# Attention of a hybrid layer: value products and row sums taken by three key tiles instead of by one

## The reference

```python
def _block_attention(q, k, v):
    qb = jnp.moveaxis(q.reshape(B, nb, Q_BLOCK, AT_KV_HEADS, AT_GROUP, D), 1, 0)
    def one(qblk):
        s = jnp.einsum('bqkgd,bskd->bkgqs', qblk, k).astype(jnp.float32) * scale
        p = jax.nn.softmax(s, axis=-1).astype(v.dtype)
        return jnp.einsum('bkgqs,bskd->bqkgd', p, v)
```

## Time and profile before

| | |
|---|---|
| Time, median of 3 runs | 2375.9 us (2374.77 to 2378.68) |
| Profiled execution: its time / its span | 2374.82 us / 2373.0 us |
| PE busy over the span | 2295.2 us (97%) |
| DVE, ACT, POOL busy | 1426.0 (60%), 805.5 (34%), 224.7 us (9%) |
| Granted TensorE clock, mean | 0.991 of full |
| Maxima of the heads, L2476 | 1.36 us each, 64 of them |
| Loop over query tiles | from about 1161.4 to 1396.15 us of the span |

### The profile page before, as it was taken

How to read it: one execution, slowest core, us unless ns; L and a number is a source line. 1 busy time by engine, 2 the same in 40 slices (tenths; PEclk the granted TensorE clock), 3 DMA queues, 4 the chain that set the end, 5 groups by cost and what they waited for, 6 DMA issues and landing times. The chain is left out here.

```text
span 2373.0 us, 43700 instructions
## 1 busy us (share of the span) xinstructions
PE 2295.2 (97%) x17959; PEld 2029.6 (86%) x17959; DVE 1426.0 (60%) x2212; ACT 805.5 (34%) x1398; POOL 224.7 (9%) x245
## 2 busy tenths in 40 slices
PE   6999999999999899998899999998999999999997
PEld 5887779999999889998655569877999999998886
DVE  5331266533555467665677646768676676677877
ACT  5321132213333233223344444325223222234444
POOL 0000000001110011112222101000111121120001
PEclk9999999999999999999999999999999999999999
DMA  6324632235452532214101138421222222259434
GB/s 279 120 85 182 225 112 107 100 135 202 155 173 86 198 107 87 83 66 158 44 19 48 56 112 312 154 92 59 79 104 91 76 107 91 73 183 271 129 98 124
DMA packets 126877, 295.60 MB, mean 125 GB/s; under 512 B 19808, under 2 KB 63280, under 8 KB 117376
## 3 DMA queue, kind: packets, MB, share of 16 engines
q1 hardware_dynamic: 98112, 238.67, 29.9%
q10 hardware_dynamic: 24640, 39.46, 4.5%
q0 software_dynamic: 3968, 15.21, 1.7%
HBM read 207.83 MB, written 85.53 MB: 124 GB/s over the span
## 5 line engine op out<-in xcount | busy, mean ns | idle before, releaser
L62 PE MATMUL ps<-prj_w,h_hi 128*128 128x512 f32 (+1 forms) x864 | 254.2, 378 | 4.2 <-DVE h_lo L755 4.2
L62 PE MATMUL ps<-h_hi,fill_whi 128*128 128x384 f32 x672 | 235.8, 351 | 4.7 <-ACT fill_st L1119 2.4
L62 PE MATMUL ps<-h_lo,fill_whi 128*128 128x384 f32 x672 | 226.6, 337 | 3.5 <-issue 3.5
L62 PE MATMUL ps<-wt 128*128 128x320 f32 (+2 forms) x1046 | 227.2, 327 | 2.3 <-DVE merged L3308 1.3
L62 PE MATMUL ps<-h_hi,fill_wlo 128*128 128x384 f32 x672 | 226.5, 337 | 0.0
L62 PE MATMUL ps<-ys,mergedr 128*128 128x256 f32 (+1 forms) x1056 | 219.9, 297 | 0.4 <-issue 0.4
L62 PE MATMUL ps<-zb,mergedr 128*128 128x320 f32 (+2 forms) x764 | 199.8, 326 | 4.9 <-issue 2.7
L62 PE MATMUL ps<-zb,wt 128*128 128x384 f32 (+3 forms) x758 | 200.2, 325 | 0.0
L62 PEld LDWEIGHTS ps<-prj_w,h_hi 128*128 128x128 f32 x864 | 157.3, 190 | 43.0 <-issue 10.6
L62 PEld LDWEIGHTS ps<-wt 128*128 128x128 f32 x1046 | 179.6, 189 | 16.6 <-issue 2.6
L62 PEld LDWEIGHTS ps<-ys,mergedr 128*128 128x128 f32 x1056 | 174.6, 191 | 0.7 <-issue 0.7
(11 more groups left out here) (512 smaller groups left out, 4654.1 us busy)
## 6 DMA issues: line engine op xcount, KB each, us to landing
wraw<-in_w_ffn_in SPq DMA_DIRECT2D x22, 1024.0 KB, 5.1
prj_raw<-in_w_ada SPq DMA_DIRECT2D x16, 1024.0 KB, 5.9
fill_raw<-in_w_fill SPq DMA_DIRECT2D x30, 512.0 KB, 4.4
wtf<-a_dram SPq DMA_DIRECT2D x55, 256.0 KB, 2.7
bg_dram<-fill_st ACTq DMA_DIRECT2D x72, 192.0 KB, 2.0
xf<-bg_dram POOLq DMA_DIRECT2D x24, 576.0 KB, 7.4
tok_dram<-prj_tst ACTq DMA_DIRECT2D x45, 256.0 KB, 2.1
prj_raw<-in_w_tok SPq DMA_DIRECT2D x10, 1024.0 KB, 7.3
```

The costliest lines, as they stand in the source:

```text
L62: mm = pe.matmul(out, lhs[a], rhs[b], start=first and n == 0, stop=last and n == 2, skip_group_check=onto)
```

## The change

`values` and `sums` take three key tiles per visit, at `j` = 3 (tiles 0 to 2), 6 (3 to 5) and 8 (6 to 8). All nine key tiles are summed by ones on PE; `pair_up` and `pair_sums` are gone, and the ring `pt` has 6 tiles in place of 5 and two pair buffers. `shift_scores(i + 1, j - 1)` stands straight behind the scores at `j` = 1 to 8, one at each. `spread_sums(i - 1)` moves from `j` = 2 to 6, and `shifts(i + 1, 1)` comes last in the tile, behind the last sums.

On VectorE `inverted(i - 1)` moves behind the maximum of head 0, `normed(i - 1)` behind that of head 5, `norm_b` to the tile's start, `norm_a` one tile earlier at head 5, both splits to the tile's end, `ahead` to head 5 of the last tile. A copy of the rotation table (L2433) is gone. On GpSimd the rotation comes at the tile's start, with the power for the next one behind it. SyncE issues `queries_in(i + 5)` ahead of the wait for `norm`.

```diff
-    RING = 5
-    PAIRS = 3
-    PAIR_DONE, P_DONE = (1, 2, 4), (3, 5, 6)
-    PAIR_AT = (4, 6, 8)
+    RING, TRIO = 6, 3
...
             def shifts(i, kv):
                 pe.wait_ge(sem["nm"], AH * i + G * kv + G)
                 pe.wait_ge(sem["pte"], turn(i, 2 + kv))
-                if kv == 0 and i >= 2:
+                if kv == 1 and i >= 2:
                     pe.wait_ge(sem["norm"], i - 1)
...
+            def values(i, g):
+
+                if g == 0:
                     if i:
                         pe.wait_ge(sem["evict"], i)
                     else:
                         pe.wait_ge(sem["b0ev"], 24)
+                for j in range(TRIO * g, TRIO * g + TRIO):
+                    n = NT * i + j
+                    pe.wait_ge(sem["ex"], 2 * n + 2)
+                    for kv in range(KV):
+                        mm = pe.matmul(ps[kv * HD:kv * HD + HD, OB, :], va[:, j, kv, 0:HD], pt[n % RING][:, kv, :],
+                                       start=j == 0, stop=j == NT - 1)
                 mm.then_inc(sem["pv"], 1)
...
+            def sums(n):
+
+                i, g = divmod(n, NT // TRIO)
+                if g == 0 and i:
+                    pe.wait_ge(sem["rc"], i)
+                for x in range(TRIO):
+                    mm = add(pt[(TRIO * n + x) % RING], g == 0 and x == 0, g == 2 and x == TRIO - 1)
                 mm.then_inc(sem["sums"], 1)
...
                     if more and j < 2:
                         queries(i + 1, j)
-                    if i and j == 2:
-                        spread_sums(i - 1)
+                    if more and j >= 1:
+                        shift_scores(i + 1, j - 1)
                     if more and j == 5:
                         shifts(i + 1, 0)
-                    if more and 1 <= j < NT - 1:
-                        shift_scores(i + 1, j - 1)
-                    if j:
-                        values(i, j - 1)
-                    if j in PAIR_AT:
-                        pair_sums(i, PAIR_AT.index(j))
-                    if j >= 7:
-                        sums(i, j - 1)
-                    if more and j == NT - 2:
-                        shift_scores(i + 1, AH - 1)
+                    if j == 3:
+                        values(i, 0)
+                        sums(3 * i)
+                    if j == 6:
+                        if i:
+                            spread_sums(i - 1)
+                        values(i, 1)
+                        sums(3 * i + 1)
+                    if j == 8:
+                        values(i, 2)
+                        sums(3 * i + 2)
                 if more:
                     shifts(i + 1, 1)
-                values(i, NT - 1)
-                sums(i, NT - 1)
...
             def exponentials(i, j):
                 n = NT * i + j
                 if n >= RING:
-                    o, oj = divmod(n - RING, NT)
-                    act.wait_ge(sem["pv"], n - RING + 1)
-                    if oj < 2 * PAIRS:
-                        act.wait_ge(sem["paired"], PAIRS * o + oj // 2 + 1)
-                    else:
-                        act.wait_ge(sem["sums"], (NT - PAIRS) * o + P_DONE[oj - 2 * PAIRS])
+                    act.wait_ge(sem["sums"], (n - RING) // TRIO + 1)
...
             def tile(i):
 
-                if i >= 1:
-                    inverted(i - 1)
+                if i == -1:
+                    norm_a(3)
+                if 0 <= i < NT - 3:
+                    norm_b(i + 3)
                 for h in range(AH):
                     if i < LAST:
                         shift(i + 1, h)
                     if i >= 1 and h == 0:
+                        inverted(i - 1)
+                    if i == LAST and h == 5:
+                        ahead()
+                    if i >= 1 and h == 5:
                         normed(i - 1)
-                    if i >= 0 and h in (1, 3, 5):
-                        pair_up(i, h // 2)
-                    if 0 <= i < NT - 3 and h == 2:
-                        norm_a(i + 3)
-                    if 0 <= i < NT - 3 and h == 3:
-                        norm_b(i + 3, qtab[:, i + 2])
-                    if 0 <= i + 2 <= LAST and h == 5:
-                        next_split(i + 2, 0)
+                    if 0 <= i < NT - 4 and h == 5:
+                        norm_a(i + 4)
                 if i + 2 <= LAST:
+                    next_split(i + 2, 0)
                     next_split(i + 2, 1)
-                if i == LAST:
-                    ahead()
```

More of the change, by code:

```diff
@@ L1905, in attention @@
             pt = [over(f"pt{i}", [P, KV, G * P]) for i in range(RING)]
-            pair = [over(f"pair{i}", [P, KV, G * P]) for i in range(2)]
         k2 = ph.sb("k2", [P, NT, KV, HD])
@@ L1909, in attention @@
         kpart = [ph.sb("kparthi", [P, NK, KV, 2 * HD], F32R), ph.sb("kpartlo", [P, NK, KV, H1], F32R)]
-        r1, r2 = ph.sb("r1", [P, NT - 1, KV, HD // 2]), ph.sb("r2", [P, NT - 1, KV, HD // 2])
         va = ph.sb("va", [P, NK, KV, H1])
@@ L1916, in attention @@
         qtab = ph.sb("qtab", [P, NT - 1, 4, HD // 2])
+        r1, r2 = ph.sb("r1", [P, NT - 1, KV, HD // 2]), ph.sb("r2", [P, NT - 1, KV, HD // 2])
         q = ph.sb("q", [P, AH, HD])
-        qtb = ph.sb("qtb", [P, 4, HD // 2])
         q2, qn, qr = (ph.sb(n, [P, AH, HD]) for n in ("q2", "qn", "qr"))
@@ L1932, in attention @@
         names = ("load qload const knd kpow kout ktm kte qd qpow rope cpart qtm qte csmm cmx cex cptm cpte comm cdone "
-                 "part s1 mx nm ptm pte s2 ex pv sums paired rc spread norm evict yout0 yout1 kv dve mly mlw mlhi b0y1 b0y2 b0w b0yh b0wh b0yl b0wl b0mm b0ev b0out0 b0out1 b0out2 b0out3 b0out4 b0out5 b1lo")
+                 "part s1 mx nm ptm pte s2 ex pv sums rc spread norm evict yout0 yout1 kv dve mly mlw mlhi b0y1 b0y2 b0w b0yh b0wh b0yl b0wl b0mm b0ev b0out0 b0out1 b0out2 b0out3 b0out4 b0out5 b1lo")
         sem = {n: ph.sem(n) for n in names.split()}
@@ L1989, in _ @@
             for i in range(LAST + 1):
+                if i + 5 < NT:
+                    queries_in(i + 5)
                 sp.wait_ge(sem["norm"], i + 1)
                 rows_out(i + 1)
-                if i + 5 < NT:
-                    queries_in(i + 5)
                 if i == 3:
@@ L2011, in _, with inverse_norm, rope @@
             gp.tensor_tensor(krs[:], kms[:], khalf[:], ALU.pow).then_inc(sem["kpow"], 1)
[L2012 to L2017, removed]
+            def inverse_norm(n):
+                gp.wait_ge(sem["qd"], 4 * n + 3)
                 gp.tensor_tensor(qrs[:], qms[:], khalf[:, 0:AH], ALU.pow).then_inc(sem["qpow"], 1)
+            def rope(n, e):
                 gp.wait_ge(sem["qd"], 4 * n + 4 + 4)
@@ L2021, in rope @@
                 o = qr[:].rearrange("p h (d e) -> p h d e", e=2)
-                w = lambda c: qtb[:, c, :].unsqueeze(1).broadcast_to([P, AH, HD // 2])
-                for e in range(2):
[L2024 to L2032, removed]
+                w = lambda c: qtab[:, n, c, :].unsqueeze(1).broadcast_to([P, AH, HD // 2])
+                a, b = (0, 1) if e == 0 else (2, 3)
+                gp.tensor_tensor(u1[:], x[:, :, :, 0], w(a), ALU.mult).then_inc(sem["rope"], 1)
+                gp.tensor_tensor(u2[:], x[:, :, :, 1], w(b), ALU.mult).then_inc(sem["rope"], 1)
+                gp.wait_ge(sem["rope"], 6 * n + 3 * e + 2)
+                gp.tensor_tensor(o[:, :, :, e], u1[:], u2[:], ALU.subtract if e == 0 else ALU.add).then_inc(sem["rope"], 1)
+                gp.wait_ge(sem["rope"], 6 * n + 3 * e + 3)
+            inverse_norm(0)
+            for n in range(2):
+                inverse_norm(n + 1)
+                for e in range(2):
+                    rope(n, e)
+            inverse_norm(3)
+            for i in range(LAST + 1):
+                if i + 2 <= LAST:
+                    rope(i + 2, 0)
+                    rope(i + 2, 1)
+                if i + 3 <= LAST:
+                    inverse_norm(i + 4)
         def turn_queries(pe, kv, bank):
@@ L2161, in values @@
                         pe.wait_ge(sem["b0ev"], 24)
-                for kv in range(KV):
-                    mm = pe.matmul(ps[kv * HD:kv * HD + HD, OB, :], va[:, j, kv, 0:HD], pt[n % RING][:, kv, :],
-                                   start=j == 0, stop=j == NT - 1)
+                for j in range(TRIO * g, TRIO * g + TRIO):
[4 more added lines that the diff above has]
+                                       start=j == 0, stop=j == NT - 1)
                 mm.then_inc(sem["pv"], 1)
@@ L2171, in add @@
                                        start=first and kv == 0, stop=last and kv == KV - 1)
-                mm.then_inc(sem["sums"], 1)
[L2174 to L2183, removed]
+                return mm
+            def sums(n):
[4 more added lines that the diff above has]
+                    mm = add(pt[(TRIO * n + x) % RING], g == 0 and x == 0, g == 2 and x == TRIO - 1)
+                mm.then_inc(sem["sums"], 1)
             def spread_sums(i):
@@ L2188, in spread_sums @@
```

(16 more changed lines are left out.)

## The result

| | before | after |
|---|---|---|
| median of the runs, us | 2375.34 (4 runs, 2373.34 to 2378.68) | 2407.24 (4 runs, 2403.64 to 2411.2) |
| ratio, with its 95% interval | | 1.0133 (1.0119 to 1.0148) |
| profiled execution, us (span) | 2374.82 (2373.0) | 2411.2 (2409.4) |
| mean granted clock of the span | 0.991 | 0.985 |
| first scores of the loop to the end of its last sums, us | 234.35 | 271.96 |

The changed kernel is 31.9 us slower by the medians and 36.4 by the two profiled executions; the profiled one after is the slowest of its four runs. The loop alone is 37.6 us longer. What lies ahead of it and behind it is 1.2 us shorter together: the loop starts 0.46 earlier, and 976.1 us follow it instead of 976.85.

What follows compares the result with a forecast made beforehand. PE's written order was taken to bound the loop: 2.1 for tile 0, 19.4 for tiles 1 to 6 and 4.8 for tile 7 made +26.3, so 2374.8 + 26.3 = 2401 us; range 2389 to 2410, its own 2394 to 2408.

Steps and rivals of the forecast that it cites:

- the sum: Attention loop: +2.1 for tile 0, +19.4 for tiles 1 to 6, +4.8 for tile 7, so +26.3 us.
- the walk of waits: PE's order in a steady tile, start by start: five waits for maxima of 3.9 us, tile 33.4 instead of 30.2.
- a slow clock at 2408: Rival: the clock falls as PE waits some 4 us per tile and idles in tile 7; 2408, chance 0.03.
- The bound and the mechanism: Attention loop: PE's written order sets the time; head scores without value products between them wait for maxima, 2.2 us cycle.
- Tile 0: First loop tile, without reciprocal or spread: 31.5 us from its opening transposes, tile 1 starting 2.1 later.
- A steady tile: Tiles 1 to 6: 33.42 us each, together +19.4 over the former 181.12.
- The prediction's list beside its walk: Steady tile, 33.4 from 30.2: waits 3.9, restarts 0.5, opening 0.4, against 0.9 less work and 0.35 formerly waited.
- The pieces: PE prices in the loop: inner value product 0.88, sums 0.46, 0.46 and 0.55, visit of three about 4.2 us.
- The covers: Remaining VectorE work, GpSimd's 6 us and moved SyncE issues stay hidden; the opening waits 0.4 for ScalarE's copy.
- Tile 7: Last tile, no head scores: PE waits for exponentials, 28.7 us instead of 23.86, so +4.8.
- The rest: Outside the attention loop nothing moves; the loop's gain or loss goes into the total whole.
- The clock: Attention loop: a fall of PE's granted clock was a rival at 0.03, since no row of the loop showed it.

Runs made afterwards that it cites:

- the kernel with pairs: Against the changed kernel: four pairs back on VectorE, five sums, value visits of 1, 3, 3, 2, heads spread, last tile ordered as before; 2371.13 us, ratio 0.9986.
- the run with the wait filled: The changed kernel with five 512-column matmuls, product thrown away, added ahead of head 2 in tiles 1 to 6; 2406.94 us, ratio 1.0129.
- the reciprocal first: The changed kernel with the reciprocal of the row sums moved ahead of the maximum of head 0; 2398.33 us, ratio 1.0106.
- the heads apart: The changed kernel with head scores spread: five at j = 1, 3, 4, 6, 7, heads 2, 5, 7 inside visits; 2387.94 us, ratio 1.006.
- the one with another tile 7: The changed kernel with value products one key tile at a time in the last query tile alone, spread at j = 2 there; 2400.19 us, ratio 1.0104.

## Why the prediction came out as it did

It forecast 2401 and slower; 2407.24 is slower by a fifth more than that (31.9 us against 26.3 in the sum). Only part of the closeness is merit. Without the clock the loop would have grown by 25.0 us (below), to 2400, so the walk of waits was right almost to the microsecond. That 2407.24 still lies inside 2394 to 2408, by 0.8, is luck: that range was meant for spacing and restarts, not for the clock, which took 12.6 us in the profiled execution. The wider 2389 to 2410 takes in a slow clock at 2408, an estimate of mine for tile 7 alone. No run shows that term; in its place the profiled execution showed falls in five tiles, 12.6 us together and 4.9 of them in tile 7 (below). Step by step:

- *The bound and the mechanism: right.* Five waits for maxima a tile were forecast for five intervals, 3.9 us, the longest 1.67 behind head 1. The view lists 28 in seven tiles, four a tile; the fifth, from head 4 to 5, is too short to be drawn as idle time. Counted from starts (0.24 behind the last matmul of the scores) the five of tile 2 are 0.67, 1.50, 0.72, 0.23 and 0.63, together 3.75 (forecast 0.66, 1.67, 0.68, 0.19 and 0.68, together 3.88); the weight side waits 28.2 us in all, 4.0 a tile. The experiments gave prices: reciprocal 0.8, order of the heads 2.0 with the reciprocal's in it.
- *Tile 0: right.* 31.5 walked, 31.47 measured, +2.10.
- *A steady tile: right within 0.2.* 33.42 walked, 33.24 where the clock held. Over six tiles that is 1.1 less than the sum had. The prediction's list beside its walk doesn't add up: 30.2 with 3.9, 0.5 and 0.4 more and 0.9 and 0.35 less is 33.75, 0.3 above the walk. The work that falls away is the item too small there: from starts, and with 0.5 of restarts taken off, tile 2 has 28.5 us of work against 29.7 before (0.1 of restart off), 1.2 less and not 0.9. The sum goes by the walk, which has it right.
- *The pieces: right.* An inner value product was taken at 0.88; from the visit shown of tile 2, (1239.55 - 1236.82 - 1.01) / 2 = 0.86. Three sums take 1.44 (1239.55 to 1240.99), as 0.46 + 0.46 + 0.55 = 1.47. The visit is 4.17 to 4.18, and 4.12 behind the spread. A lone value product takes 0.15 more from start to start than an inner one (1.01 against 0.86); no run here shows what that difference is made of.
- *The covers: right.* `normed`, `norm_b`, splits and GpSimd hold up nobody, and the wait for ScalarE's copy at the opening is 0.31 in the view and 0.46 from starts (0.4 forecast), though the kernel with pairs shows how near `normed` is: behind one maximum more it costs 1.5 us a tile.
- *Tile 7: the walk fits, the clock not in it.* 28.7 was walked and 33.36 measured. PE waits for exponentials six times, 3.9 us in all. What the clock cost is below, and without it some 28.5 are left, which no run shows by itself.
- *The rest: right within 1.2 us.* Nothing outside the loop is slower.
- *The clock: wrong, and this is the mis-sized term.* The forecast gave it a chance of 0.03, with the reason that no row of the loop before showed it. No row of the loop could: before, PE had no wait there like those that the walk itself had just found. But the trace of before shows it 20 us ahead of the loop, where PE has such waits. Behind waits of 1.41 and 0.69 us head scores take 1.10 instead of 0.79, the granted clock is 0.50 from 1140.97 to 1144.39, and the window of that stretch stands at 0.97:

```profile
1139.34 0.66 PE L2036 MATMUL ps<-ident,att_qpart 128*128 128x128 f32 x4 [1.41 <-DVE att_y L2469]
1140.69 1.10 PE L2131 MATMUL ps<-att_kthi,att_qt 128*128 128x384 f32 x3 [0.69 <-ACT att_qt L2304]
...
1100.00:1161.00 61.00, 54.68 (x332) 51.33 (x330) 35.70 (x64) 23.54 (x48) 13.60 (x15) 0.97 0.23 75
```

What it cost, in the profiled execution of the changed kernel:

```profile
1201.42 1.33 PE L2134 MATMUL ps<-att_kthi,att_qt 128*128 128x384 f32 x3 [1.34 <-DVE att_mx L2470]
1202.68 3.67 PE L2167 MATMUL ps<-att_pt,att_va 128*64 128x512 f32 x12
...
1372.27 1.33 PE L2134 MATMUL ps<-att_kthi,att_qt 128*128 128x384 f32 x3 [1.34 <-DVE att_mx L2470]
1373.53 5.27 PE L2167 MATMUL ps<-att_pt,att_va 128*64 128x512 f32 x12
...
1405.92 0.80 PE L2153 MATMUL ps<-att_qt,att_kthi 128*128 128x512 f32 x1 [0.79 <-ACT att_pt L2317]
...
1407.92 5.14 PE L2167 MATMUL ps<-att_pt,att_va 128*64 128x512 f32 x12
...
1418.68 0.50 PE L2153 MATMUL ps<-att_qt,att_kthi 128*128 128x512 f32 x1 [1.55 <-ACT att_pt L2317]
```

and windows of the changed kernel around the fall of tile 1, around the same wait in tile 2, and at the falls of tile 6 and the first of tile 7 (the clock is the third number from the end):

```profile
1200.00:1201.40 1.40, 0.09 (x1) 0.00 (x0) 1.37 (x2) 0.80 (x2) 0.00 (x0) 0.88 0.00 0
1201.40:1204.80 3.40, 3.38 (x9) 1.51 (x11) 1.67 (x3) 0.00 (x0) 0.00 (x0) 0.55 0.00 0
1204.80:1207.70 2.90, 2.90 (x56) 1.53 (x52) 0.00 (x0) 0.00 (x0) 0.00 (x0) 1.00 0.03 6
1234.60:1236.10 1.50, 0.17 (x1) 0.00 (x0) 1.47 (x3) 0.87 (x2) 0.00 (x0) 1.00 0.00 0
1236.10:1240.90 4.80, 4.79 (x63) 2.50 (x63) 1.65 (x3) 0.00 (x0) 0.00 (x0) 1.00 0.02 3
...
1372.20:1378.70 6.50, 6.43 (x15) 2.06 (x15) 1.68 (x4) 0.00 (x0) 0.00 (x0) 0.51 0.00 0
1406.00:1412.90 6.90, 6.90 (x16) 2.32 (x16) 3.48 (x3) 3.54 (x5) 0.00 (x0) 0.52 0.00 0
```

In a fall the granted clock is 0.50 of full: from 1201.07 to 1204.46 in tile 1, from 1371.74 to 1378.55 in tile 6, from 1405.87 to 1412.68 and from 1419.52 to 1422.92 in tile 7. The windows at 0.51 to 0.55 hold little besides. The three value products of a visit then take up to 5.27 us instead of 2.80. Tiles 1, 3, 5 and 6 stand 1.4, 1.6, 1.6 and 3.1 above 33.24, which is 7.7. In tile 7 the first visit with the scores ahead of it runs from 1405.92 to 1412.99, 7.07 us, where the same pieces take 1.04 + 2.73 at the full clock, so 3.3 more; a second fall, from about 1419.5, costs 1.6 by the same count (scores, spread and value products, 5.8 where 4.2 is due). Together 12.6. The walk as measured without it is 2.1 for tile 0, 18.3 for tiles 1 to 6 (6 x 33.24 - 181.12) and 4.6 for tile 7 (28.5 - 23.86), so 25.0; and 25.0 + 12.6 is the 37.6 by which the loop grew. These two parts were split from the loop's own time, so their sum is no check. For tiles 1 to 6 the check is the run with the wait filled, with tiles of 33.24 to 33.29 at a clock of 1.00; for tile 7 there is only the count of pieces. Another look at the size: length times (1 - clock) over the windows of tiles 1, 3, 5, 6 and 7 is 13.5, of which what fell into waits cost nothing. A slower clock in tile 7 is worked out from pieces here; that tile in the changed order was seen at the full clock in no run. The four runs of after have mean granted clocks of 0.985, 0.987, 0.987 and 0.988 at 2411.2, 2407.19, 2407.28 and 2403.64 us: the higher the mean clock, the shorter the run. Only the first has a trace, so how many falls the others had, and what the clock cost in the median run, isn't shown.

That the idle time is the cause is shown on both sides: filling it, and shortening it to 0.5, took away every fall from tile 1 to tile 6, and value products between the scores of tile 7 took away those there. Each of these rests on one profiled execution.

## What to carry to other kernels

When a reordering leaves TensorE waiting for a round trip through another engine, walk the order with that latency (here 2.2 us: 0.80 for the scores, 1.36 for the maximum, 0.06 to go on) and keep that much other work in each interval; an engine that is idle on average doesn't shorten it (VectorE was busy 17.66 us of the 33.23 of tile 2), and one long instruction between two maxima on its queue adds to it (the reciprocal of 1.76 us cost 0.8 per tile). Look through the whole trace, not the loop alone, for a slow clock behind waits, and price each wait of a length that had a fall behind it here (1.34 us, and 0.80 and 0.79 in tile 7) with a possible fall: a fall cost 1.4 to 3.3 us here, and not every wait had one. Joining narrow work saves little (0.15 for a value product behind another, and two borders of 0.09 with full-width work), less than the 0.46 of an added sum, so leave the sums of pairs on an engine with time to spare: the joined order with four pairs on VectorE, heads spread out, is the one that won.

## What the runs showed of the hardware that was not expected

- TensorE's granted clock fell from 1.00 to 0.50 of full behind single waits of 1.33 or 1.34 us (tiles 1, 3, 5, 6), of 1.48 (the kernel with pairs, tile 4), and in tile 7 behind two of 0.80 and 0.79 with 1.2 us of scores between them, and behind one of 1.55. In the changed kernel and in the runs with the reciprocal first, the wait filled and the heads apart, tile 7 stands at 0.84 or 0.85 alike. It stayed at 0.50 for 3.4 us (tile 1) or 6.8 us (tile 6, the first of tile 7).
- The same wait didn't always do it: 1.34 us in tiles 2 and 4 of the changed kernel, and 1.40 to 1.50 in the other tiles from 1 to 6 of the kernel with pairs, left the clock at 1.00, and the tiles hit differ between two kernels with the same waits (1, 3, 5 and 6 in the changed kernel; 3, 5 and 6 in the one with another tile 7). What decides between two equal waits no run here tried, and it stays open.
- Waits up to 0.57 us, four a tile, never did it in tiles 1 to 6 of the kernel with the reciprocal first.
